# Two blocks on one core: wide moving operands in the 256-token feed-forwards, and values held still in the 64-row heads

## The reference

```python
# layers 0 and 1
out_a = chunk_gmlp(a_z, a_ws[i], a_bs[i])                       # part A
out_b = window_attn_latent(q_b, k_b, v_b, k_bc, v_bc, b_sink[i])  # part B: 8 heads of 64, 2 key heads, softmax with a sink
out_c = (rms_norm(o_c, c_subln[i]) * (1 - lam_init))            # part C: 4 heads, difference of two softmaxes
x = x + g1 * (concat([out_a, out_b, out_c]) @ w_out[i])
x = x + g2 * conv_ffn(modulate(rms_norm(x, norm2_g[i]), sh2, sc2), ...)   # conv over 3 tokens on gate and value
# layers 2 and 3
x = x + gate_m * rmsnorm(latent_attention(q, k_all, v_all) @ w_o[j], g_post_mix)   # layer 2; layer 3: pooling
u = h @ w_up; gate, val = u[..., :D_FF_2], u[..., D_FF_2:]
gate = gp[:, :-2]*conv_w[0] + gp[:, 1:-1]*conv_w[1] + gp[:, 2:]*conv_w[2] + conv_b   # conv on the gate alone
y = (silu(gate) * val) @ w_down
```

## Time and profile before

| | before |
|---|---|
| median of three runs | 1653.2 us |
| the profiled execution | 1649.52 us, span 1647.7 us |
| granted TensorE clock, mean | 0.983 |
| TensorE matmuls busy | 1573.1 us (95%), 10648 instructions |
| VectorE busy | 1009.7 us (61%) |
| ScalarE busy | 811.1 us (49%) |
| GpSimd busy | 94.7 us (6%) |
| moved by DMA | 287.51 MB, 174 GB/s in the mean |

### The profile page before, as it was taken

One profiled execution on the slowest core, in us unless ns is written; L12 is line 12 of the kernel. 1 busy time (PEld: TensorE's weight loads), 2 busy tenths in 40 slices (PEclk: granted clock), 3 DMA queues, 4 the chain that ended last, 5 costly groups with the idle time before them and its releaser, 6 DMA issues.

```text
span 1647.7 us, 29630 instructions
## 1 busy us (share of the span) xinstructions
PE 1573.1 (95%) x10648; PEld 1357.9 (82%) x10648; DVE 1009.7 (61%) x1706; ACT 811.1 (49%) x1422; POOL 94.7 (6%) x146
## 2 busy tenths in 40 slices
PE   3999999899999999899999999899999999799997
PEld 1777777688888888698889999697799998599997
DVE  3453775665565477666678875654566744776654
ACT  3342773444444322455656655435455544565543
POOL 0021000000000111010000000030100001000000
PEclk9999999999999999899999999999999999899998
DMA  9666105323332587352168658432865578646563
GB/s 382 245 211 205 39 2 197 109 90 102 94 97 85 170 268 256 118 142 83 28 243 278 181 183 315 145 129 103 331 243 179 174 246 289 249 130 184 173 167 112
DMA packets 76865, 287.51 MB, mean 174 GB/s; under 512 B 9024, under 2 KB 12608, under 8 KB 67056
## 3 DMA queue, kind: packets, MB, share of 16 engines
q1 hardware_dynamic: 60832, 190.23, 36.4%
q0 software_dynamic: 15952, 96.18, 15.6%
HBM read 282.44 MB, written 1.05 MB: 172 GB/s over the span
## 4 chain that ended last, share of the span: by engine, by line
PE 89%; DVE 5%; DMA 3%; ACT 1%; issue 1%; SPq 0%; DVEq 0%; ACTq 0%
PE B L1669 23%; PE B L1671 23%; PE B L1670 22%; PE B L1690 4%; PE B L1915 3%; PE B L1863 2%; DVE NORM L1181 2%; DMA MW<-in_wmod 2%; DMA RAW<-in_wup 1%; PE B L1682 1%; PE B L1684 1%; PE B L1683 1%; PE B L1886 1%; DVE HL L1171 1%; PE B L1785 1%; PE B L1804 1%
## 5 line engine op out<-in xcount | busy, mean ns | idle before, releaser
L1669 PE MATMUL B<-HH,WHI 128*128 128x256 f32 (+1 forms) x1872 | 600.7, 321 | 26.0 <-DVE HL L1171 20.5
L1670 PE MATMUL B<-HL,WHI 128*128 128x256 f32 (+1 forms) x1872 | 591.6, 316 | 0.0
L1671 PE MATMUL B<-HH,WLO 128*128 128x256 f32 (+1 forms) x1872 | 591.6, 316 | 0.0
L1080 DVE TENSOR_TENSOR WLO<-RAW,WHI 128x1024 fp32r<-128x1024 f32 (+1 forms) x376 | 412.7, 1100 | 221.8 <-ACT WHI L669 221.0
L669 ACT ACTIVATE WHI<-RAW 128x1024 fp32r<-128x1024 f32 (+1 forms) x376 | 359.5, 959 | 219.6 <-PE B L1671 197.3
L1669 PEld LDWEIGHTS B<-HH,WHI 128*128 128x128 f32 x1872 | 359.7, 192 | 68.6 <-issue 26.3
L1671 PEld LDWEIGHTS B<-HH,WLO 128*128 128x128 f32 x1872 | 360.3, 192 | 21.5
L1670 PEld LDWEIGHTS B<-HL,WHI 128*128 128x128 f32 x1872 | 360.6, 193 | 19.9
L1669 PE MATMUL B<-MIDH,WHI 128*128 128x256 f32 (+1 forms) x704 | 218.7, 311 | 0.0
L1671 PE MATMUL B<-MIDH,WLO 128*128 128x256 f32 (+1 forms) x704 | 218.3, 310 | 0.0
L1670 PE MATMUL B<-MIDL,WHI 128*128 128x256 f32 (+1 forms) x704 | 218.3, 310 | 0.0
(11 more groups left out here) (210 smaller groups left out, 1631.2 us busy)
## 6 DMA issues: line engine op xcount, KB each, us to landing
RAW<-in_wup SPq DMA_DIRECT2D x176, 512.0 KB, 3.7
GWR<-in_wmod POOLq DMA_DIRECT2D x33, 1024.0 KB, 8.3
RAW<-in_wdn SPq DMA_DIRECT2D x64, 384.0 KB, 3.3
RAW<-in_wproj SPq DMA_DIRECT2D x44, 512.0 KB, 4.5
RAW<-in_wdn SPq DMA_DIRECT2D x64, 320.0 KB, 3.6
GWA<-in_wmod POOLq DMA_DIRECT2D x19, 1024.0 KB, 5.9
WINV<-in_wmod POOLq DMA_DIRECT2D x32, 512.0 KB, 5.3
RAW<-in_wout SPq DMA_DIRECT2D x24, 512.0 KB, 3.6
```

The lines of the kernel that those rows point to most:

```text
L1080: v.tensor_tensor(WL[s][:, 0:kts, :], RAW[s][:, 0:kts, :], WH[s][:, 0:kts, :].bitcast(F32), ALU.subtract).then_inc(lo_done, 1)
L1669: mm(bank[:, 0:t], wh, a, start=first and k == ks[0], stop=False)
L1670: mm(bank[:, 0:t], wh, b, start=False, stop=False)
L1671: ins = mm(bank[:, 0:t], wl, a, start=False, stop=stop and k == ks[-1])
```

## The change

Feed-forwards over 256 tokens. High and low activations now lie in one tile each (`HHL`, `MID`). A new `products_apart` takes a weight tile with two matmuls: the high weight against high and low activations in one 512-column matmul, whose halves land in columns 0 to 255 and 256 to 511 of the bank, and the low weight against the high activation in columns 0 to 255. It is used in the up projections of layers 2 and 3 and for output tiles 0 to 6 of the down projections of layers 1, 2 and 3. The halves are then added: in the up projection ScalarE copies columns 256 to 511 to `Y` and VectorE adds the others (`sum_halves`), for gate and for value; the taps, the silu and the product then work from `Y`, and VectorE's order of weight splits changes. In the down projection VectorE adds the halves to `X` one after the other (layer 1) or reduces them into `Y`, from where ScalarE squares and copies (layers 2, 3).

Attention of layers 0 and 1, "b" slots. Values (128 keys x 64 columns) are the stationary operand and the turned probabilities (128 queries) stream; the two heads of a slot write rows 0 to 63 and 64 to 127 of the bank, so the output is already feature-major, and the transposes L1932 go. The reciprocal sums now have to lie along the columns: VectorE computes them (`sums`), GpSimd spreads them (`RX`), TensorE turns them (`turn_sums`, four transposes for each `qt`), ScalarE copies them (`RBS`), VectorE multiplies (`group`). The copies to `HH` and `HL` move from behind the last slots into the loop, but for the last `qt`, whose `mix_lo` stands before `means`. The first output parts are begun on banks 0, 1 and then 2, 3.

```diff
-        HH = sb("HH", [P, KT, 512], F32R)
-        HL = sb("HL", [P, KT, 512], F32R)
+        HHL = sb("HHL", [P, 2, KT, 512], F32R)
+        HH, HL = HHL[:, 0], HHL[:, 1]
...
-        MIDH = {t: sb(f"MIDH{t}", [P, FT, t], F32R, at=w0) for t in (256, 512)}
-        MIDL = {t: sb(f"MIDL{t}", [P, FT, t], F32R, at=w0 + FT * t * 4) for t in (256, 512)}
+        MID = {t: sb(f"MID{t}", [P, 2, FT, t], F32R, at=w0) for t in (256, 512)}
+        MIDH, MIDL = {t: MID[t][:, 0] for t in MID}, {t: MID[t][:, 1] for t in MID}
...
+        def wide_up(l):
+            return l >= 2
+        def wide_tile(l, m):
+            return TT[l] == 256 and not (isinstance(m, int) and m == KT - 1)
...
+            def spread_sums(l):
+                for qt in range(TT[l] // P):
+                    k = total([4, 2], l) + qt
+                    gp.wait_ge(r_ready, k + 1)
+                    gp.tensor_copy(RX[:].rearrange("p h (e d) -> p (h e) d", e=2),
+                                   SM[:, 64 + 8 * qt:72 + 8 * qt].unsqueeze(2).broadcast_to((P, 8, 64))
+                                   ).then_inc(rx_ready, 1)
...
                 def mix_hi(j):
                     out, src = mix_out(l, j, HH)
-                    act.wait_ge(mt_mm, mt_base[l] + j + 1)
+                    if j < nq:
+                        act.wait_ge(group_out, total(NGROUP, l) + 2 * j + 2)
+                    else:
+                        act.wait_ge(ct_mm, total([2, 1], l) + j - nq + 1)
                     if MIXES[l][j][0] == "c":
                         ins = act_f(out, src, ACT.Copy, scale=LAM[:, l, 3:4])
                     else:
                         ins = act_f(out, src, ACT.Copy)
                     ins.then_inc(m_hi, 1)
+                def sums_out(qt):
+                    i = SLOTS[l][min(8 * qt + 8, len(S) - 1)]["n"][-1]
+                    act.wait_ge(rbs_mm, total([4, 2], l) + qt + 1)
+                    act_f(RBS[:], banks[2 + (i + 1) % 2][:], ACT.Copy).then_inc(rbs_ev, 1)
                 for j in range(len(S) + 2):
                     if j >= 2:
                         s = S[j - 2]
                         for i in s["n"]:
                             copy_pt(l, i, s["keys"][1] - s["keys"][0])
+                    if j >= 10 and j % 8 == 2:
+                        sums_out(j // 8 - 1)
+                    if j >= 12 and j % 8 == 4:
+                        mix_hi(j // 8 - 1)
                     if j < len(S):
                         exps(S[j])
                     if j == 1:
...
                         ahead(LATE_SPLITS[l][j])
                     if j in (7, 8):
                         gated_hi(j - 7)
-                for j in range(nq - 1):
-                    mix_hi(j)
+                sums_out(nq - 1)
                 mean_roots()
                 for j in range(nq - 1, NMIX[l]):
...
                         act.wait_ge(mid_lo, pg + 1)
                         act.wait_ge(blk_used, 4 * n4 + s0 + 1)
-                        act_f(yg, banks[s0][:, 0:t], ACT.Identity, scale=g_w(1), bias=cbg).then_inc(affine, 1)
-                        split(n4, s0, last)
-                        act.wait_ge(drained, TUP0[l] + 4 * i + s0 + 1)
+                        if wide_up(l):
+                            act_f(Y[:, s0, 256:512], banks[s0][:, 256:512], ACT.Copy).then_inc(apart, 1)
+                            split(n4, s0, last)
+                            act.wait_ge(drained, TUP0[l] + 4 * i + s0 + 1)
+                        act_f(yg, Y[:, s0, 256:512] if wide_up(l) else banks[s0][:, 0:t], ACT.Identity, scale=g_w(1),
+                              bias=cbg).then_inc(affine, 1)
+                        if wide_up(l):
+                            act.wait_ge(blk_used, 4 * n4 + s0 + 2)
+                            act_f(Y[:, s0 + 1, 256:512], banks[s0 + 1][:, 256:512], ACT.Copy).then_inc(apart, 1)
+                        else:
+                            split(n4, s0, last)
+                        if wide_up(l):
+                            act.wait_ge(tapped, FT * (l - 2) + pair + 1)
+                        else:
+                            act.wait_ge(drained, TUP0[l] + 4 * i + s0 + 1)
                         act_f(yg, yg, ACT.Silu).then_inc(silu_done, 1)
                         act.wait_ge(blk_used, 4 * n4 + s0 + 2)
                         if IS_L[l]:
...
                                 VEC[:, bass.ds(VCOL[l, "cb"] + FT + pair, 1)]
                             act_f(yv, banks[s0 + 1][:, 0:t], ACT.Identity, scale=v_w, bias=cbv).then_inc(affine, 1)
                         split(n4, s0 + 1, last)
-                        if IS_L[l]:
-                            act.wait_ge(prod, pg + 1)
...
                             if s == 3 and not IS_L[l]:
-                                tile_squares(l, "down", 2 * i + a, a, banks[a])
-                                o = TDOWN0[l] + 2 * i + a
+                                src = banks[a][:, 0:256]
+                                if wide_tile(l, 2 * i + a):
+                                    act.wait_ge(drained, TDOWN0[l] + 2 * i + a + 1)
+                                    src = Y[:, a, 256:512]
+                                tile_squares(l, "down", 2 * i + a, a, src)
                                 yb = YB[:, 2 * i + a, :] if isinstance(i, int) else YB[:, bass.ds(2 * i + a, 1), :]
-                                src = banks[a][:, 0:256] if isinstance(i, int) else \
-                                    banks[a][:, 0:256].unsqueeze(1)
+                                if not isinstance(i, int):
+                                    src = src.unsqueeze(1)
                                 gate = DER[:, 3, 2 * i + a, 0:1] if isinstance(i, int) else \
                                     DER[:, 3, bass.ds(2 * i + a, 1), 0:1].rearrange("p a b -> p (a b)")
-                                act_f(yb, src, ACT.Copy, scale=gate).then_inc(drained, 1)
+                                act_f(yb, src, ACT.Copy, scale=gate).then_inc(
+                                    yb_done if wide_tile(l, 2 * i + a) else drained, 1)
...
-                        k, u0 = qt, s["at"] - 6
-                        dve.wait_ge(sink_exp, k + 1 + (4 if l else 0))
-                        link(v.tensor_tensor(SM[:, 32 + 8 * k:40 + 8 * k], SM[:, 8 * k:8 * k + 8],
-                                             SM[:, 384 + u0:392 + u0], ALU.add))
-                        link(v.reciprocal(SM[:, 64 + 8 * k:72 + 8 * k], SM[:, 32 + 8 * k:40 + 8 * k]))
-                        v.tensor_tensor(OT[:, qt, 0:512].rearrange("p (h c) -> p h c", c=64),
-                                        bank[:, 0:512].rearrange("p (h c) -> p h c", c=64),
-                                        SM[:, 64 + 8 * k:72 + 8 * k].unsqueeze(2).broadcast_to((P, 8, 64)),
-                                        ALU.mult).then_inc(group_out, 1)
+                        dve.wait_ge(rbs_ev, total([4, 2], l) + qt + 1)
+                        v.tensor_tensor(OT[:, qt, 0:512], bank[:, 0:512], RBS[:], ALU.mult).then_inc(group_out, 1)
...
+                def sums(s):
+                    k, u0 = s["qt"], s["at"] - 6
+                    dve.wait_ge(sink_exp, k + 1 + (4 if l else 0))
+                    link(v.tensor_tensor(SM[:, 32 + 8 * k:40 + 8 * k], SM[:, 8 * k:8 * k + 8],
+                                         SM[:, 384 + u0:392 + u0], ALU.add))
+                    v.reciprocal(SM[:, 64 + 8 * k:72 + 8 * k], SM[:, 32 + 8 * k:40 + 8 * k]).then_inc(r_ready, 1)
...
+                    if j >= 9 and j % 8 == 1:
+                        sums(S[j - 2])
+                    if j >= 13 and j % 8 == 5 and j // 8 - 1 < nq - 1:
+                        mix_lo(j // 8 - 1)
...
-                    if j == len(S) + 2:
-                        for k in range(nq - 1):
-                            mix_lo(k)
+                mix_lo(nq - 1)
                 means()
-                for k in range(nq - 1, NMIX[l]):
+                for k in range(nq, NMIX[l]):
...
+                        def sum_halves(k):
+                            dve.wait_ge(apart, NUP * (l - 2) + 2 * pair + k + 1)
+                            v.tensor_tensor(Y[:, s0 + k, 256:512], banks[s0 + k][:, 0:256], Y[:, s0 + k, 256:512],
+                                            ALU.add).then_inc(drained, 1)
                         yg, yv = Y[:, 2 * j, 0:t], Y[:, 2 * j + 1, 0:t]
-                        taps(0)
-                        lo_split(n4 + 1, s0, DOWN_KT[s0] if last else 8)
-                        if IS_L[l]:
+                        if wide_up(l):
+                            sum_halves(0)
+                            if j:
+                                lo_split(n4 + 1, 1, DOWN_KT[1] if last else 8)
+                            elif not (isinstance(i, int) and i == 0):
+                                lo_split(n4, 3, 8)
+                            y, b = Y[:, s0, 0:256], Y[:, s0, 256:512]
+                            dve.wait_ge(affine, affine_base(l) + pair + 1)
```

(61 more changed lines are left out.)

83 lines of the change are left out of this document (51 added, 32 removed).

## The result

The changed kernel took 1642.96 us in the median of seven runs (1637.35 to 1649.04), beside 1653.2 for the kernel before in seven runs of the same sessions (1650.37 to 1655.72). The ratio is 0.994, 95% interval 0.9926 to 0.9955: 10.2 us faster (7 to 12), where 25.0 were forecast. The direction was right, the size was not: the time lies above the 1621 to 1635 of the forecast, at the upper edge of the range that took in the rivals (1620 to 1643).

The account below looks back on a forecast made before the run. TensorE was taken to bound the kernel; 15.2 us from the feed-forwards and 9.8 from the attentions sum to 25.0, so 1653.2 becomes 1628.2 us. Forecast 1621 to 1635 (62 in 100); range with rivals 1620 to 1643.

Parts of the forecast that it names:

- What bounds the kernel: Whole kernel: TensorE sets the time, busy 95% of the span, with 89% of the chain on it.
- Part 1, the tile: Feed-forwards: a weight tile falls from 360 to 347 ns, 13 ns on each of 1166 tiles, 15.2 us.
- Rival (b): Feed-forwards: the wide matmul is no cheaper than two narrow ones, 0 to 3 us gained, 1640 to 1643; 8 in 100.
- The broken operand at nothing: Feed-forward wide matmuls: reading the operand in two separate runs of 256 costs nothing.
- rival (c): Up projections of layers 2 and 3: VectorE's closed loop, forecast at 5.58 us a pair, binds from 5.70; 10 in 100.
- Part 2, the slots: Attentions of layers 0 and 1: 0.91 us saved per long "b" slot, 0.52 per short; ceiling 18.7, together 9.8 us.
- what is late next: Attention pairs: ScalarE or VectorE limits the gain to 0.4 to 0.88 us a long pair, 5.0 us a layer.
- The short slots: Layer 0's eight 256-key pairs: 1.0 us gained after 0.5 for reciprocals through GpSimd; bounds -1 to +3.
- The ends: Ends of the attentions: layer 0 saves 0.5 us, layer 1 loses 1.7 as TensorE waits for the means.
- (a): Attentions give nothing because ScalarE and VectorE eat the saving: 1638, with a few us of loss 1642; 13 in 100.
- (d): All covers hold and the attentions give nearly their ceiling: 32 us gained, 1621 and below; 4 in 100.
- (e): Attention values: the two heads' matmuls follow one another, 120 ns an instruction instead of 64; about 1640; 3 in 100.

Follow-up runs that it names:

- the feed-forwards alone: Kernel before with only the wide feed-forward tiles, attentions unchanged: 1644.72 us, ratio 0.9954 to the kernel before.
- by twos: Changed kernel with weight tiles taken in twos (wide, wide, narrow, narrow): 1638.67 us, ratio 0.9917 to the kernel before.
- experiment 3: Changed kernel with high and low activations of the down projections side by side, one run of 512: 1642.95 us, ratio 0.9942 to the kernel before.
- Experiment 6: Changed kernel with TensorE turning a "b" slot's probabilities ahead of the previous slot's values: 1640.66 us, ratio 0.993 to the kernel before.
- experiment 9: Changed kernel with turns ahead of values and four buffers of turned probabilities instead of two in layers 0 and 1: 1634.35 us, ratio 0.9888 to the kernel before.
- experiment 7: Changed kernel without GpSimd's spread, the reciprocals' transposes and ScalarE's copy; VectorE multiplies by another tile: 1641.34 us, ratio 0.993 to the kernel before.
- experiment 10: Changed kernel with roots and means ahead of the last reciprocals' copy and low half, and a relaxed wait: 1641.08 us, ratio 0.991 to the kernel before.
- the attentions alone: Changed kernel with the wide feed-forward tiles switched off, only the 64-row heads kept: 1649.07 us, ratio 0.9978 to the kernel before.
- in whole blocks: Changed kernel with all wide matmuls of a weight block ahead of its narrow ones, the bank's last staying wide: 1639.12 us, ratio 0.9919 to the kernel before.

## Why the prediction was right or wrong

**What bounds the kernel:** right. TensorE stayed full in layer 3's feed-forward, and what its matmuls lost, the stretch lost: 352 x 7.5 and 154 x 6.8 ns make 3.7 us, and it is 3.7 us shorter.

**Part 1, the tile: the mechanism right, the term too large.** 13 ns a tile was forecast, 7.5 measured in the up projection and 6.8 in the down. Over 704 and 462 tiles that is 8.4 us; the stretches give 3.7 + 3.3 + 0.9 = 7.9, with layer 2 taken from the profile in which its weights come in time, and the feed-forwards alone 7.6, for 15.2. The failing step is "the three fit columns / 2.4 GHz plus 13 ns": those distances were all read within runs of one width, and a wide one among narrow ones costs 236 ns and not 227. Undoing the alternation gives 348 to 351 and comes near the forecast's 347. Rival (b), that a wide matmul costs as much as two narrow ones, would be 240: the truth lay between, nearer to (b) in the alternation and nearer to the forecast by twos. The Trainium skill, "TensorE: Matmul & The Clock Gate", section "Back-to-back issue gap", has the gap N/2.4 + 2.5 ns, by which the wide form would save 2.5 ns a tile. The trace doesn't agree: 7 to 8 ns in alternation, 9 to 12 by twos.

**The broken operand at nothing:** right (experiment 3).

**VectorE's closed loop, rival (c):** didn't bind. TensorE busy 60.00 of 60.00 us, VectorE 50.0, which is 4.7 a pair of 5.64 us, where 4.8 was said. The adjacent terms, the reduction in the down projection and the later loads, show no stall in layer 3 either. In layer 2, where the forecast put late loads at nothing within 0 to 2 us, they cost about 3.5 us in three of fourteen profiles; that the moved splits are the cause isn't shown.

**Part 2, the slots: the saving a little too large in the forecast, what is late next wrong.** The attentions gave 3.8 us in the stretches, for 9.8. The table above says where the 6.0 are missing: 2.6 and 2.5 in the long pairs of the two layers, 1.9 in the short ones, while the two ends came out 0.3 and 0.7 better than forecast.

The failing step is the one headed "what is late next": I set a pair at the largest busy time of any engine, 5.2 to 5.7. The forecast has no term for a chain that goes to and fro between engines: exponentials, transposes, copy, values, with two buffers between copy and values. Its pairs are 5.5 to 5.6 with no engine full. Experiment 6 moved the wait within this chain; experiment 9 took the buffers out and brought a long pair of the second block to 5.27 us, TensorE's own work. But it left the first block at 5.62, where ScalarE's sequence holds the pair, and of its 4.2 us at most 1.2 + 0.4 lie in pairs with scores; the other 1.9 in layer 1 lie in the last two pairs, for which the forecast had 0.88 each. So the chain through the buffers is shown for the second block only, and the first block's sequence is read from the trace and not tested.

Two terms beside it were too small or too large. The values save 0.8 us a slot and not 0.91, since the forecast compared two pieces of the chain and not the distances of starts: 16 x 0.1 = 1.6 us. In the short slots, where a values group with its 8 matmuls now takes 0.60 us for 0.94 (before from 227.78 to 228.72, after from 231.61 to 232.21), it is 0.34 for 0.52. And the way of the reciprocals was dearer by 1.5 us (experiment 7).

**The short slots** had a term of +1.0 within bounds of -1 to +3, and gave -0.9: just inside the bounds, on the wrong side of nothing. Without the reciprocals' way their eight pairs take 28.5 us, as before the change, so it costs them 0.9 where 0.5 was said; with four buffers they take 28.7; what eats the shorter values beyond that stands on the chain, which runs over VectorE's minima and the low half of `HHL`, but no run took these out.

**The ends:** right in the path, priced a little too dear. In layer 1 the chain from the last values to the "c" part goes through exactly the steps that the forecast lists (reciprocals turned, copied, table load, copy, low half, means), in 5.1 us for 4.9, and 1.61 us of idle TensorE stand there for "1 to 2 us". The end lost 1.0 us against before, for -1.7, and 1.8 came back when the means went first (experiment 10). Layer 0's end gained 0.8, for 0.5.

**Rivals.** In the time (b), 1640 to 1643, comes nearest, and (a), attentions worth nothing, at 1638 to 1642, next to it; neither is what happened. The feed-forwards gave 7.6 us where (b) allows 0 to 3, and the attentions 3.6 where (a) has none. (d) is excluded by the same 3.6, (e) by 1.03 us for a slot's values, 64 ns an instruction. The time still falls into the range, 0.04 us below its upper end. That is luck: two terms missed by about 7 and 6 us in the same direction, and the range was wide only for rivals with other mechanisms.

**Outside the sum.** The stretch with layer 2's attention and output projection, from the first scores to the sums behind the projection, took 62.6 us in all fifteen profiles of changed kernels and 63.8 or 63.9 in the two of before, and so it does where only one part is changed. In the kernel before a gap of 1.13 us stands at its end behind VectorE's last sum, which waited behind the split of a first up block; in the attentions alone that split is done earlier. The arrival of this block is earlier, and why was not tried. With it the stretches of the result's table gain 7.9 + 3.8 + 1.2 = 12.9 us, and the late start takes 2.6 of them back, which would leave the 10.2 of the medians; this is a sum of stretches from few profiles, no run shows it. The pooling stretch took 46.2 and 49.0 us in the kernel before and 46.8 to 52.2 in the others. The granted clock differs there from profile to profile: from 1400 to 1450 us it is 0.80 and 0.67 in the two of before, 0.67 and 0.77 in the two of the changed kernel, which had 52.2 and 48.5. So this stretch tells nothing of the change.

## What to carry to other kernels

Read a matmul's price in the neighbourhood that it will have: a distance from a run of equal widths doesn't hold in an alternation of widths, and the order can be changed at little cost (twos instead of ones, with a later first matmul where operands are just being made). Compare prices by distances of starts on both sides, not by pieces of the chain. When the bounding engine's work shrinks in a pipeline of several engines, the new period is not the next largest busy time but the longest closed chain through the buffers; count its hand-overs, and see which buffer closes it. A stretch that differs by 3.5 us between two profiles of one kernel must be known as such before an edit is credited or blamed.

## What the runs showed of the hardware

The alternation: 512 and 256 columns in turn take 352 to 354 ns a pair, by twos 348 (down projection) to 351 (up), in whole blocks 349, all at a granted clock of 1.00. A wide operand in two runs of 256 with 22 KB between them costs the same as one run of 512 (353 against 353). Matmuls with 64 stationary columns of float32, on the two halves of the output rows in turn, take 1.03 us for 16 from start to next start, 64 ns each, both in the heads and in the gated mix (starts at 158.15 and 159.18 in the kernel before). In the kernel of experiment 9, where the two heads of a slot can read differently named buffers, one sees that the two halves run side by side, with starts 10 ns apart:

```profile
191.54 0.32 PE L2034 MATMUL B<-PTX,VV 128*64 128x128 f32 x1 [0.29 <-ACT PTS L880]
191.55 0.32 PE L2034 MATMUL B<-PTS,VV 128*64 128x128 f32 x1
191.70 0.27 PE L2034 MATMUL B<-PTX,VV 128*64 128x128 f32 x1
```

And the weights' arrival in layer 2's down projection, late or in time from one execution of the same kernel to the next, at a DMA share of 0.86 to 0.87 in both.
